# A two-block network kernel: the first projection in three passes inside the RWKV turns, half of the modulation slabs moved to the up stage

## The reference, cut to what matters

```python
h = rmsnorm(x, g[0])
z = h @ w_in                      # 2048 x 6016: 47 tiles of 128 columns
za, zb, zc = split(z)             # attention | spatial gating | RWKV
oa = dilated_attention(qkv(za))   # tiles 0..17
ob = spatial_gating(zb)           # tiles 18..25
oc = rwkv7_time_mix(zc)           # r 26..31, k 32..37, v 38..43, low-rank inputs 44..46
y = concat([oa, ob, oc]) @ w_out
...
up = h @ ffn_w_up                 # 88 tiles, convolution, gelu, then ffn_w_down
```

```python
sh, sc, g = split(silu(c) @ w_mod[l] + b_mod[l])   # 96 slabs in all (l = 0, 1)
```

## Time and profile before

| | us |
|---|---|
| median of 3 runs | 3125.95 |
| lowest and highest | 3122.44, 3127.62 |
| span of the profiled execution, first to last instruction | 3116.5 |
| PE busy in it | 3010.5 (97%) |
| DVE busy | 1616.9 (52%) |
| ACT busy | 1307.2 (42%) |
| moved by DMA | 509.68 MB |

### The profile page before, as it was taken

How to read it: one execution, slowest core, us unless ns; L and a number is a source line. 1 busy time by engine, 2 the same in 40 slices (tenths; PEclk the granted TensorE clock), 3 DMA queues, 4 the chain that set the end, 5 groups by cost and what they waited for, 6 DMA issues and landing times.

```text
span 3116.5 us, 48446 instructions
## 1 busy us (share of the span) xinstructions
PE 3010.5 (97%) x19528; PEld 2531.8 (81%) x19528; DVE 1616.9 (52%) x2513; ACT 1307.2 (42%) x2036; POOL 17.8 (1%) x35
## 2 busy tenths in 40 slices
PE   7999999899889999999999999999999999999997
PEld 7966666689768888888888887788888998889896
DVE  5444444545366667674454323554553574247754
ACT  4322112343455555554443224444442472255544
POOL 0000000000000000000000000000000000000000
PEclk9999999999989999999999999999999999999998
DMA  6677787544435555555553222222233442234343
GB/s 231 207 296 307 307 317 306 196 142 162 149 121 188 188 182 184 187 173 180 183 193 113 95 95 81 81 73 100 82 108 126 163 163 95 95 119 149 136 163 109
DMA packets 73751, 509.68 MB, mean 164 GB/s; under 512 B 8309, under 2 KB 8449, under 8 KB 19585
## 3 DMA queue, kind: packets, MB, share of 16 engines
q1 hardware_dynamic: 70416, 486.08, 44.2%
q0 software_dynamic: 3184, 21.40, 1.8%
HBM read 503.23 MB, written 6.55 MB: 164 GB/s over the span
## 4 chain that ended last, share of the span: by engine, by line
PE 91%; DVE 4%; ACT 2%; DMA 2%; issue 1%; SPq 0%; ACTq 0%; DVEq 0%
PE bank L712 25%; PE bank L656 15%; PE bank L655 7%; PE bank L864 6%; PE bank L1334 5%; PE bank L1336 5%; PE bank L1335 5%; PE bank L881 2%; PE bank L960 2%; DMA high_f<-in_w_in 2%; PE bank L753 2%; PE bank L754 1%; PE bank L755 1%; PE bank L1020 1%; PE bank L1372 1%; PE bank L1276 1%
## 5 line engine op out<-in xcount | busy, mean ns | idle before, releaser
L2102 DVE TENSOR_TENSOR ring_f32r<-ring_f,high_f32r 128x1024 fp32r<-128x1024 f32 (+1 forms) x690 | 771.5, 1159 | 765.9 <-ACT high_f32r L1509 762.4
L1509 ACT CAST high_f32r<-ring_f 128x1024 fp32r<-128x1024 f32 (+1 forms) x690 | 655.3, 998 | 889.0 <-PE bank L712 528.6
L656 PE MATMUL bank<-hyz_f32r,high_f32r 128*128 128x512 f32 x2112 | 741.6, 399 | 7.4 <-DVE hyz_f32r L2102 7.4
L712 PE MATMUL bank<-hyz_f32r,high_f32r 128*128 128x256 f32 (+1 forms) x2688 | 654.8, 327 | 6.8 <-DVE ring_f32r L2102 3.7
L655 PE MATMUL bank<-hyz_f32r,ring_f32r 128*128 128x256 f32 x2008 | 564.1, 281 | 1.9 <-DVE hyz_f32r L2102 1.0
L712 PE MATMUL bank<-hyz_f32r,ring_f32r 128*128 128x256 f32 (+1 forms) x1520 | 505.5, 333 | 0.0
L712 PEld LDWEIGHTS bank<-hyz_f32r,high_f32r 128*128 128x128 f32 x2688 | 452.2, 190 | 51.0 <-issue 6.2
L656 PEld LDWEIGHTS bank<-hyz_f32r,high_f32r 128*128 128x128 f32 x2112 | 391.2, 188 | 95.6 <-issue 8.1
L655 PEld LDWEIGHTS bank<-hyz_f32r,ring_f32r 128*128 128x128 f32 x2008 | 379.7, 189 | 7.3 <-DVE ring_f32r L2102 1.6
L1334 PE MATMUL bank<-hyz_f32r,high_f32r 128*128 128x512 f32 (+1 forms) x1024 | 359.1, 351 | 2.8 <-DVE ring_f32r L2102 2.8
L1336 PE MATMUL bank<-hyz_f32r,ring_f32r 128*128 128x512 f32 (+1 forms) x1024 | 344.8, 337 | 0.0
(11 more groups left out here) (395 smaller groups left out, 3479.5 us busy)
## 6 DMA issues: line engine op xcount, KB each, us to landing
ring_f<-in_w_in SPq DMA_DIRECT2D x135, 1024.0 KB, 5.0
ring_f<-in_w_mod SPq DMA_DIRECT2D x96, 1024.0 KB, 9.1
ring_f<-in_w_up SPq DMA_DIRECT2D x88, 1024.0 KB, 5.0
ring_f<-in_w_out SPq DMA_DIRECT2D x56, 1024.0 KB, 5.0
ring_f<-in_w_down SPq DMA_DIRECT2D x64, 704.0 KB, 4.0
high_f<-in_w_in SPq DMA_DIRECT2D x24, 1024.0 KB, 5.1
ring_f<-in_w_kv SPq DMA_DIRECT2D x8, 1024.0 KB, 4.9
ring_f<-in_w_q SPq DMA_DIRECT2D x4, 1024.0 KB, 5.0
```

What stands on the lines that cost most here:

```text
L656: last = mm(bank, hi, pair(x_hi, x_lo), start=start, stop=stop)
L712: last = mm(bk[(t0 + j) % banks][:, 0:width], w[:, c], x[:, k], start=(k == 0 and w is hi and x is rhs.hi), stop=(k == KC - 1 and w is lo))
L1509: act.copy(w_hi[p % 2][:, half], slot[s % SLOTS][:, half]).then_inc(w_high, 1)
L2102: return v.tensor_tensor(out, in0, in1, op)
```

## The change

- `in1` now counts 47 tiles, all with three passes, in a new order: 44, 45, 46 and the r, k, v tiles of turn 0 first (`IN1_EARLY` = 6), then in turns 0 to 5 seven, seven, seven, seven, six and six tiles; the 47th is filler of the attention, as the last tile was before. The r, k, v tiles of turn i+1 are computed in turn i and lie in six rotating places of `Z`.
- ACT casts and DVE subtracts half slabs one by one (`in1_cast`, `in1_lowered`), at places written out within the turns: some 14 halves in each. A half is cast as soon as the tile two before it has been read to the half (`in1_half`). Three ring slots hold projection slabs, the fourth (`MOD_SLOT`) the modulation slabs.
- Only 48 modulation slabs stay in the turns, eight in each, one after every 14 chunks (12 in turns 4 and 5). PE turns the summed rows in turns 2 and 4 and in the last tile.
- The other 48 are loaded by the POOL queue into two buffers in `H[0]` and read between the tiles of the up stage (`UP_MODS`), one slab in about two of three tiles.
- The filler asked for is larger (12.0 + 8.0 us ahead of the chain instead of 2.4 + 6.5, 1.15 instead of 0.85 between the steps of the inverse), and PE starts turn i+1's first matmuls (`ups_matmuls`) right behind the group norm of turn i.
- The ACT and DVE turns and the up stage of PE are no longer loops. Buffers move (RWKV scratch, `mod_c`, squares of `memT`); `G` is loaded in two halves, the second after the last turn.

```diff
-IN1_US, MOD_US = 0.434, 0.87
-BESIDE_TILES, BESIDE_SLABS = 23 + 6 * 4, 23 + 6 * 16
+IN1_US, MOD_US = 0.36, 0.95
+IN1_SLOTS, MOD_SLOT = 3, 3
+IN1_EARLY = 6
+IN1_FIRST, IN1_COUNT = (6, 13, 20, 27, 34, 40), (7, 7, 7, 7, 6, 6)
+IN1_LAST = 46
+MOD_EVERY = (14, 14, 14, 14, 12, 12)
+TURN_MODS = 8
+UP_MODS = [2 + 3 * k // 2 for k in range(16)] + [32 + 3 * k // 2 for k in range(16)] + [62 + 4 * k // 3 for k in range(16)]
+UP_TURNED = (29, 61, 85)
...
+            def mod_slab(n):
+                if n:
+                    sp.wait_ge(S("mod_read"), n)
+                sp.dma_start(slot[MOD_SLOT], d["w_mod"][n, :, :]).then_inc(mod_slot, 16)
...
+            for i in range(C_TILES):
+                for n in range(1, KC * IN1_COUNT[i] + 1):
+                    k, m = IN1_FIRST[i] + n // KC - 1 + IN1_SLOTS, TURN_MODS * i + n // MOD_EVERY[i]
+                    if n % KC == 0 and k <= IN1_LAST:
+                        in1_tile(k)
+                    if n % MOD_EVERY[i] == 0 and m < TURN_MODS * C_TILES:
+                        mod_slab(m)
...
+            pool.wait_ge(rhs_split, RHS0["up"] + 4)
+            for n in range(48):
+                if n >= 2:
+                    pool.wait_ge(S("mod_read"), 48 + n - 1)
+                if n:
+                    pool.wait_ge(S("up_mod_loaded"), 16 * n)
+                pool.dma_start(up_mod[n % 2], d["w_mod"][48 + n, :, :]).then_inc(S("up_mod_loaded"), 16)
...
+            def in1_steps(k):
+                r, b = RHS["in1"], bk[k % 2][:, 0:T]
+                hi, lo = w_hi[k % 2], w_lo[k % IN1_SLOTS]
+                for n in range(KC):
+                    if n == 0:
+                        pe.wait_ge(gemm_free, k - 1)
+                    if n % (KC // 2) == 0:
+                        pe.wait_ge(in1_low, 2 * k + 2 * n // KC + 1)
+                    c = slice(n * P, (n + 1) * P)
+                    mm(b, hi[:, c], r.hi[:, n, 0], start=(n == 0), stop=False)
+                    mm(b, hi[:, c], r.lo[:, n, 0], start=False, stop=False)
+                    last = mm(b, lo[:, c], r.hi[:, n, 0], start=False, stop=(n == KC - 1))
+                    if n == KC // 2 - 1:
+                        last.then_inc(in1_half, 1)
+                    elif n == KC - 1:
+                        last.then_inc(gemm_done, 1)
+                    yield IN1_US
...
             def projection1(i):
...
+                steps = 0
+                for k in range(IN1_FIRST[i], IN1_FIRST[i] + IN1_COUNT[i]):
+                    for us in in1_steps(k):
+                        yield us
+                        steps += 1
+                        if i in (2, 4) and steps == 4:
+                            mod_turned(i // 2 - 1, 7, mod_row)
+                        if steps % MOD_EVERY[i] == 0:
+                            turn_mod(TURN_MODS * i + steps // MOD_EVERY[i] - 1)
+                            yield MOD_US
...
-            gemm3("up")
+            for j in range(TILES["up"]):
+                gemm3("up", j, 1, opening=(j == 0))
+                if j in UP_MODS:
+                    up_mod_matvec(48 + UP_MODS.index(j))
+                if j in UP_TURNED:
+                    g = 3 + UP_TURNED.index(j)
+                    pe.wait_ge(S("mod_out"), g + 1)
+                    mod_turned(g, 5, up_mod_row)
...
+            def in1_cast(n=1):
+                for _ in range(n):
+                    k, half = in1_part(casts[0])
+                    act.wait_ge(w_in_slot[k % IN1_SLOTS], 16 * (k // IN1_SLOTS + 1))
+                    if k >= 2:
+                        act.wait_ge(gemm_done if casts[0] % 2 else in1_half, k - 1)
+                    act.copy(w_hi[k % 2][:, half], slot[k % IN1_SLOTS][:, half]).then_inc(in1_high, 1)
+                    casts[0] += 1
...
                 act.copy(gv, bk[3][:, 0:T]).then_inc(S("rw_sig"), 1)
+                if i in (2, 4):
+                    mod_row_copied(i // 2 - 1, 7, mod_row)
+                    mod_copied(i // 2 - 1, 7)
+                if i:
+                    in1_copied(first - 1)
+                    in1_cast()
+                in1_cast()
+                in1_copied(first)
+                in1_cast(2)
                 act.wait_ge(S("rw_kkss"), i + 1)
...
                 step(ts(kn, k_, gp[:, KK:KK + 1]))
+                in1_lowered(2 if i else 1)
                 tt(tmp, kn, kn).then_inc(S("rw_kksq"), 1)
...
                 stt(bonus, r_, gp[:, RK:RK + 1], k_).then_inc(S("rw_bonus"), 1)
+                in1_lowered(2)
                 dve.wait_ge(S("rw_kkn"), i + 1)
```

More of the change, by code:

```diff
@@ L345, in build @@
         h1.take(A_HEADS * T)
-        G = Z[:, 26:26 + A_HEADS]
+        G_AT = (26, 32)
+        G = [Z[:, G_AT[h // 6] + h % 6, :] for h in range(A_HEADS)]
         g_line = h1.take(384)
@@ new lines, in _, with mod_matvec, mod_turned @@
+            in1_tile(4)
+            in1_tile(5)
+            def mod_matvec(n, bank, slab):
+                for m in range(4):
+                    last = mm(bk[bank][32 * m:32 * m + 32, :], mod_c[:, n % KC, :], slab[:, m * 512:(m + 1) * 512],
+                              start=(n % KC == 0), stop=(n % KC == KC - 1))
+                last.then_inc(S("mod_read"), 1)
+            def mod_turned(g, bank, row):
+                pe.wait_ge(S("mod_row"), g + 1)
+                for b in range(4):
+                    last = mm(bk[bank][:, 8 * b:8 * b + 8], row[:, b * P:(b + 1) * P], mod_sel, start=True, stop=True)
+                last.then_inc(S("mod_turned"), 1)
@@ L2190, in _, with in1_lowered @@
                 rhs_low("in1", q)
-            low("in1", 0)
-            low("in1", 1)
-            lows("in1", 2, 4)
+            lowered = [0]
+            def in1_lowered(n=1):
+                for _ in range(n):
+                    k, half = in1_part(lowered[0])
+                    dve.wait_ge(in1_high, lowered[0] + 1)
+                    tt(w_lo[k % IN1_SLOTS][:, half], slot[k % IN1_SLOTS][:, half], w_hi[k % 2].bitcast(F32)[:, half], ALU.subtract
+                       ).then_inc(in1_low, 1)
+                    lowered[0] += 1
+            in1_lowered(10)
+            dve.wait_ge(gemm_free, 3)
+            v.memset(lora[0], 0.0)
+            step(v.memset(lora[1], 0.0))
+            for n in range(3):
+                z = Z[:, 44 + n, :]
+                tt(tmp[:, 1:T], z[:, 0:T - 1], z[:, 1:T], ALU.subtract)
+                step(ts(tmp[:, 0:1], z[:, 0:1], -1.0))
+                step(stt(z, tmp, vec("mulo")[:, n:n + 1], z, op1=ALU.add))
+            dve.sem_inc(S("early_made"), 1)
+            in1_lowered(2)
             dve.wait_ge(S("lam_line_made"), 1)
@@ L2318, in turn @@
                 add_tt().then_inc(S("inv_dve"), 1)
+                in1_lowered()
                 multiplied(5)
@@ L2369, in turn @@
                 dve.wait_ge(S("rw_y"), i + 2)
-            with dve.Fori(0, C_TILES - 1) as i:
-                step.loop(i, 26)
+            for i in range(C_TILES):
                 turn(i)
-            step.end(C_TILES - 1)
-            turn(C_TILES - 1, True)
             dve.sem_inc(rhs_made, 1)
```

395 lines of the change are left out of this document (220 added, 175 removed).

## The result

The changed kernel takes 3134.04 us (median of five runs, 3130.68 to 3138.08) against 3124.44 us for the kernel before on the same chip: a ratio of 1.0035, with a 95% interval of 1.0024 to 1.0046. The forecast was 3113 us, a gain of 12.8 us; the time moved the other way, +9.6 us.

A forecast was written before the change was run, and what follows sets the result against it. PE was taken to bind everywhere. Terms of -99.2 ahead of the turns, +33.7 in the turns, -1.2 for the last tile and +53.9 in the up stage gave -12.8 us, so 3113 us, range 3086 to 3143.

The forecast's parts named there:

- Part 1: Ahead of the turns: 17 tiles leave, the third tile waits less, the first turn's matmuls wait slightly: -99.2 us.
- Turns of 74.2 us: Turns 0, 1 and 3: RWKV matmuls and gaps, filler chunks, eight modulation slabs and a slab wait total 74.2 us each.
- (a): Group norm's last step to key square: DVE needs 13.1 us, PE has 14.6 us of filling; costed at nothing.
- (c): Between steps of the inverse: PE's filler and matmuls cover DVE's answer and added half-slab work; costed at nothing.
- (b): Key root to prepared operands: ready at 23.4 to 24.5 us, PE there at 24.6; covered, costed at nothing.
- The slab waits: PE waits for modulation slabs in their one slot: 0.5 us once a turn, 2.5 in turn 4, 2.0 in turn 5.
- 75.0 in turn 2, which has the transposes: Turn 2 takes 75.0 us, as it includes transposes of a summed row, priced at 0.81 us.
- rival 2: In the turns, ACT holds the key root behind a cast waiting for its slab: 3137 to 3161 us; chance 0.16.
- The forecast's 80.9: Turn 5: 34.3 us staying, 34.6 chunks, 8.5 slabs, 1.5 uncovered answers and 2.0 slab waits, 80.9 us.
- The lone slab: A modulation slab read alone costs 1.06 us, between bounds 0.853 and 1.19; 48 in the up stage, with transposes, +53.9.
- Rival 3: Up stage: slabs on POOL's queue land late and PE waits, 3170 or 3290 us; chance 0.05.
- The 9.5 us between span and median: Whole kernel: the median lay 9.5 us above the profiled span of 3116.5; carried over, giving 3125.95 - 12.8 = 3113.

The follow-up runs named there:

- the first run: Changed kernel, with ACT copying the modulation row at the head of turns 2 and 4, before its waits there: 3119.93 us, ratio 0.9990.
- the fixes: Changed kernel with four edits together: row copied first, bias broadcast two tiles later, turn 5's low halves earlier, up slabs in pairs: 3104.09 us, ratio 0.9934.
- the root-first run: Changed kernel, with ACT taking the key root between the two casts there, not behind the second, in all six turns: 3133.94 us, ratio 1.0031.

## Why the prediction was wrong

The direction was missed because four stalls that the prediction had costed at nothing, or not seen, made the six turns 21 us longer than forecast, where the whole forecast gain was 12.8. The up stage, 5.5 us over its forecast, would not have turned the sign alone. Point by point:

- **Part 1** held: -100.6 for -99.2.
- **Turns of 74.2 us** held where no stall fell: 74.4 and 73.2. So did the new turn's chunk price, the work of DVE and ACT (45 and 26 us for 45 and 28), and DMA near 210 GB/s. In (a) and (c) nothing was late in these two turns; at (b) PE waited 0.9 us in turn 1. With the fixes, turns 0 to 5 come to 73.0, 73.0, 74.2, 73.2, 74.9 and 81.3, forecast 74.2, 74.2, 75.0, 74.2, 74.8 and 80.9.
- **The slab waits** of 0.5 us a turn were 0.6 and 0.4 in turns 1 and 3. In turns 4 and 5, where 2.5 and 2.0 had been summed, they were 1.0 and 0.4. So 3.1 us of overestimate hide part of the stalls in these two turns.
- **"75.0 in turn 2, which has the transposes"**, and the 0.8 us for them in turn 4, are the steps that failed most. They charge the transposes as work and ask nothing of the wait in front of them. The change had moved them from the tenth chunk of a turn's last tile, where PE waited for nothing (368.40 in the earlier trace rows), to the fourth chunk of the next turn, while ACT's copy went behind ACT's first waits there. Each cost 4.25 us of waiting and some low clock behind it: +5.6 each, and the first run won 11.7 us in these two turns by moving the copy alone (7.0 in turn 2; 4.7 in turn 4, whose last 7.5 us had a clock of 0.50 in that run and 1.00 in the changed kernel).
- **Turn 0** was costed like turns 1 to 3. The broadcast on GpSimd's queue stayed at about 75 us while the turn moved under it, and the prediction never placed it in time: +6.6, and 6.9 came back.
- **Point (b) and rival 2** had the right place in turn 5 and the wrong engine. ACT's root was late as described, and cost nothing, for DVE had the two low halves in front of it: PE waited 4.19 us at the products, where the forecast had nothing. The forecast's 80.9 became 83.9, and 78.0 in the run that moved the two halves.
- **The lone slab** was mis-sized: 1.19 us measured for 1.06 taken. The upper bound worked out from the earlier trace rows was 1.19. The reason to stay below it, that part of both gaps belongs to any semaphore wait, was wrong: a pair of slabs has two such waits and pays the 0.35 us once. With the transposes it makes +59.4 for +53.9.
- **Rival 3** was rightly small. On GpSimd's queue 1 MB landed in 6.9 us (median of the 48), between the bounds of 5.0 and 8.3, and PE never waited.
- **No term for the clock.** The prediction's prices are all at full clock. Behind each of the four waits of 4.2 to 5.5 us PE's matmuls took up to twice their time, so such a stall costs more than its length: 7.0 us for a wait of 4.25 in turn 2, 6.9 for 5.5 in turn 0.
- **The 9.5 us between span and median** that the forecast carried over is no constant: it is 2.0 us for the changed kernel. It was right to carry it, but for another reason, the quick execution that was profiled.

What stays open is why the clock falls where it does in stretches that no edit touched, and it moves whole runs by several us:

- **Turn 4 with its stall** lasted 79.1 to 80.4 us in six traces and 82.5 to 84.5 in four. In the four the clock was 0.50 to 0.61 in its last 8 us (turn 4's row of short waits for the chunk states, 0.4 to 1.2 us each); in the other six it was 0.99 or 1.00 there, with the same waits.
- **Turn 5 with its stall** lasted 81.7 to 84.4 us.
- **The attention stage** took 75.6 to 75.9 us in the changed kernel and in five of the runs (bias read moved, slabs in pairs, no slabs, one matmul of four, 128 columns), and 72.0 to 72.2 in the other six, the root-first run among them, which changed nothing there. Its low clock fell on another stretch in the two groups (0.66 between 20 and 30 us into the stage in the short ones, 0.75 and 0.76 between 10 and 30 in the long).
- **The part behind the down projection** took 1488.7 us in the changed kernel and 1488.7 to 1492.7 in the runs, with no edit in it. By the clock record of the traces it is by and large the longer, the longer the clock was at 1.2 GHz in it: 16.6 us in the shortest, 28 in the longest.

In the first run the attention's 3.3 us and this part's 3.0 about cancel. In the runs with the broadcast later and the low halves earlier the attention was 3.4 and 3.5 us shorter and this part 4.0 longer. So the size of a single gain is good to some 2 to 5 us in turns 4 and 5; what the runs show there is the order of the waits.

## What to carry to other kernels

Where a tuned order is cut anew, ask of every wait that moves who stands behind it: program order on the engine that releases it sets its cost, not that engine's busy share. Follow the triggers that count tiles, too: the broadcast tied to the eighth tile stayed where it was in time, and the work beside it became another. And when a late result is found, look for the consumer's own order before repairing the producer: here two repairs of the producer gave nothing, and moving two instructions of the consumer took 3.7 to 5.9 us out of the turn.

## What the runs showed of the hardware

- Four float32 matmuls of 512 columns, each filling its own 32 output rows, cost 0.853 us together, the same as one of them. The Trainium skill's page "TensorE: Matmul & The Clock Gate", in "Part 3: Packing small matmuls — row/col tiling", says that matmuls at different positions of the array run at the same time; the runs agree (811.1 us with one of four for 811.9, and 0.55 us for a visit with four of 128 columns, which one behind the other would stream as many columns as one of 512, 1.17 us).
- Going from full-width fp32r matmuls to 32-wide float32 ones and back costs 0.35 us, and two slabs in a row pay it once (803.5 for 811.9 us, 24 pairs). The Trainium skill's page "TensorEngine Tiling (Array Packing)", in "Key Properties", says that a change of tiling mode drains TensorE and gives no time; these runs are in line with it and put 0.35 us on the two changes, though none changed the mode alone.
- A wait of 4.2 to 5.5 us was followed by matmuls at half clock (1.88 us for 0.96, 1.93 for 1.06). Shorter waits were or were not: at the products of turn 5 one of 1.67 us was not (0.67 us for the sixteen), one of 2.34 us was (clock 0.50 from 455.0 to 458.4 us), and the row of waits of 0.4 to 1.2 us at the end of turn 4 was in some runs.
- 48 loads of 1 MB on GpSimd's queue beside SyncE's own, 260 GB/s together in the up stage for 185 before, cost PE nothing beyond the reading of the slabs (53.6 us less without 45 of them, 45 times the 1.19 of a visit).
